# The order of query blocks in the prompt attention of a decoder kernel: 7, 3, 6, 2, 5, 1, 4, 0 instead of 0 to 7

## What is computed

```python
def prompt_attend(q_lat, q_pe, ckv, kpe):
    b, h, s, r = q_lat.shape
    nb = s // Q_BLOCK
    ...
    def block(args):
        qlb, qpb, blk = args
        q_pos = blk * Q_BLOCK + jnp.arange(Q_BLOCK)
        sc = jnp.where(key_pos[None, :] <= q_pos[:, None], mla_scores(qlb, qpb, ckv, kpe), NEG_INF)
        p = jax.nn.softmax(sc, axis=-1).astype(ckv.dtype)
        return jnp.einsum('bhst,btr->bhsr', p, ckv)
```

## Time and profile before

| | us |
|---|---|
| median of 3 runs | 2984.7 (2984.61 to 2985.17) |
| the profiled execution | 2993.13 |
| its span | 2991.0 |
| prompt attention, first scores to last copy | 424.6 to 588.7 |
| TensorE busy | 2811.2 (94% of the span) |
| VectorE, ScalarE, GpSimd busy | 1741.4, 1077.3, 1212.0 |
| mean granted clock of TensorE | 0.973 |

### The profile page before, as it was taken

How to read it: one execution, slowest core, us unless ns; L and a number is a source line. 1 busy time by engine, 2 the same in 40 slices (tenths; PEclk the granted TensorE clock), 3 DMA queues, 4 the chain that set the end, 5 groups by cost and what they waited for, 6 DMA issues and landing times. The chain is left out here.

```text
span 2991.0 us, 60241 instructions
## 1 busy us (share of the span) xinstructions
PE 2811.2 (94%) x24873; PEld 2558.0 (86%) x24873; DVE 1741.4 (58%) x3025; ACT 1077.3 (36%) x2174; POOL 1212.0 (41%) x835
## 2 busy tenths in 40 slices
PE   6999999999999989999999997898989999999996
PEld 4887776666668989999999987877989999999996
DVE  5341245588864876666652276975586666664234
ACT  4511026522225633333320145765553333331111
POOL 2411137733325544444431145784544444433202
PEclk8999989999999999999999998998999999999998
DMA  9555400187743313232382323111232323254422
GB/s 313 185 181 195 137 22 1 52 281 273 278 155 102 118 60 102 103 107 98 102 293 104 126 83 92 43 33 50 83 100 84 109 90 115 89 213 167 148 83 83
DMA packets 232396, 377.87 MB, mean 126 GB/s; under 512 B 14523, under 2 KB 155196, under 8 KB 223669
## 3 DMA queue, kind: packets, MB, share of 16 engines
q1 hardware_dynamic: 200108, 253.95, 25.8%
q0 software_dynamic: 11776, 75.50, 7.2%
q10 hardware_dynamic: 20240, 44.57, 4.1%
HBM read 298.71 MB, written 73.28 MB: 124 GB/s over the span
## 5 line engine op out<-in xcount | busy, mean ns | idle before, releaser
L804 PE MATMUL ps<-HS,w_split 128*128 128x272 f32 x1920 | 272.3, 292 | 23.1 <-POOL w_split L1397 9.8
L804 PEld LDWEIGHTS ps<-HS,w_split 128*128 128x128 f32 x1920 | 253.1, 190 | 28.7 <-ACT sg L1061 14.3
L820 PE MATMUL ps<-HS,w_ring 128*128 128x272 f32 x1920 | 274.7, 290 | 0.0
L820 PEld LDWEIGHTS ps<-HS,w_ring 128*128 128x128 f32 x1920 | 255.4, 190 | 0.0
L2328 PEld LDWEIGHTS ps<-HS_in,w_split 128*128 128x128 f32 x1728 | 223.8, 192 | 28.7 <-issue 18.0
L1799 DVE TENSOR_TENSOR Y<-Y,ps 128x272 f32<-128x272 f32 x256 | 111.9, 437 | 224.9 <-PE ps L820 224.9
L2328 PE MATMUL ps<-HS_in,w_split 128*128 128x272 f32 x1728 | 234.8, 295 | 8.5 <-DVE HS_in L2548 8.4
L1397 POOL TENSOR_TENSOR w_split<-w_raw,w_split 128x512 fp32r<-128x512 f32 x120 | 169.9, 1429 | 156.1 <-ACT w_split L1053 156.1
L775 PE MATMUL ps<-HS,w_ring 128*128 128x272 f32 x1344 | 179.3, 294 | 18.0 <-PEq L3466 11.4
L775 PEld LDWEIGHTS ps<-HS,w_ring 128*128 128x128 f32 x1344 | 175.1, 193 | 20.3 <-POOLq L1446 11.6
L1397 POOL TENSOR_TENSOR w_ring<-w_raw,w_ring 128x512 fp32r<-128x512 f32 x40 | 61.1, 1528 | 270.0 <-ACT w_ring L1053 270.0
(11 more groups left out here) (503 smaller groups left out, 6384.2 us busy)
## 6 DMA issues: line engine op xcount, KB each, us to landing
hid_spill<-hid SPq DMA_DIRECT2D x40, 1088.0 KB, 7.4
w_mod_half<-w_mod_in SPq DMA_DIRECT2D x40, 1024.0 KB, 6.5
HS<-hid_spill ACTq DMA_DIRECT2D x32, 1088.0 KB, 10.7
w_raw<-w_ffn_gate_in SPq DMA_DIRECT2D x44, 512.0 KB, 4.1
w_raw<-w_ffn_up_in SPq DMA_DIRECT2D x44, 512.0 KB, 4.7
w_raw<-w_ffn_down_in SPq DMA_DIRECT2D x44, 512.0 KB, 4.6
x_part<-x_spill SPq DMA_DIRECT2D x54, 272.0 KB, 3.0
x_spill<-Y SPq DMA_DIRECT2D x12, 1088.0 KB, 5.6
```

What stands on the lines that cost most here:

```text
L804: ins = pe.matmul(psum(U.banks(u)[b]), part_slot(j, a)[:, k, :], token_part(n, j, e)[:, k, :], start=(j < 3 and k == 0 and i == 0), stop=( ...
L820: ins = pe.matmul(down_bank(n), slots[DOWN_SLOT[t]][:, a, d * P:(d + 1) * P], hid_cols(k, t, q)[:, e, :], start=(t == lo and j == 0), stop ...
```

## The change

The blocks within a head pair are taken from a table. The wait for the queries and keys of a head, which stood at block 0, now stands at the first block of the pair, whichever that is.

```diff
+BLOCKS = (7, 3, 6, 2, 5, 1, 4, 0)
+
+
 def stage_attention(c, cq, ckv, kq, tab, yb, qlat, qpe, first):
...
         def blk(u):
-            return u // 2 % NQ
+            return BLOCKS[u // 2 % NQ]
...
-                if b == 0:
+                if u // 2 % NQ == 0:
                     pe.wait_ge(q_roped, h + 1)
                     pe.wait_ge(pe_set, h + 1)
```

## The result

The changed kernel takes 2992.59 us in the median of 12 runs (2989.12 to 2997.64), the kernel before 2984.85 in 12 runs taken beside them (2979.38 to 2995.64). The ratio is 1.0024, 95% interval 1.0016 to 1.0032: **slower by 7.2 us, 4.8 to 9.6**. That is clear of no change, and its interval reaches to both sides of the 0.2% (6 us) named before the run. One run on each side of experiment 9 (3456.21 and 6982.73 us) fell in a slow state, and the ratio there leaves them out. The profiled execution took 2994.79 us, span 2992.7, clock 0.975; before it was 2993.13. That pair hides the loss: behind the paged stage's last maximum the program took 2107 us, where the profile of before has 2111. The same code took 2112 us in a second profile of the change. So I compare marks inside the two stages, not spans.

A forecast was written before the change was run, and what follows sets the result against it. TensorE was taken to bound the stage, other engines counting only where late. Fill +2.7, three pairs at +0.85 and drain -2.75 gave +2.5 us, so a median of 2987.2 us, range 2981 to 2993.

The forecast's parts named there:

- rival B: Next stage entered late, so GpSimd's gather of the third page group may land late: +5 to +6.5 us; chance 0.13.
- The waits of the new order: TensorE's waits at junctions 7 to 3, 6 to 2, 5 to 1, 4 to 0: 0.2 to 0.9 us each.
- The pair at +0.85: Each head pair takes about 0.85 us more, 37.5 us: waits of 3.7 to 3.8 us against 2.9 before.
- the prediction on weight loads: In a head pair, weight loads' busy share (23.74 of 36.70 us) shows nearness to the limit better than matmuls' busy time.
- The fill at +2.7: At the stage's start, transposes wait for block 7's long first normalisation: +2.7 us, or +1.7 with the clock effect.
- The drain at -2.75: In the last head pair, short blocks last let the final normalisation end 39.55 us in, not 42.3: -2.75 us.
- Sum at the gather: Fill, three pairs and drain together delay GpSimd's gather behind the last normalisation by 2.5 us.
- so this is hidden by 1.9 us: At the stage's end, entry delayed to about 595.1 us is covered by gathered pages arriving at 597.0.
- It passes whole into the next stage: The +2.5 us at the gather carries fully into the next stage, bound by TensorE after its start.
- Rival A: At the fill, TensorE's half-clock stretch ends 7 to 10 us later: +7 us, 2991.7; chance 0.13.
- Rival C: In each pair, mixed long and short blocks shrink 2.9 us of waits to about 1: -8.6 us, 2976; chance 0.09.
- Rival D: Clock falls inside the loop, one low stretch per pair: +17.5 us, 3002; chance 0.03.

The follow-up runs named there:

- experiment 9: The changed kernel with the last head pair back in the order 0 to 7: 2990.66 us against 2989.1 for the kernel before, ratio 1.0002.
- experiment 1: The changed kernel run again with no edit: 3000.28 us against 2986.36 for the kernel before, one run each.
- experiment 2: The changed kernel with the new order in the first head pair only, the others 0 to 7: 2985.43 us.
- experiment 5: The changed kernel with ScalarE's copy of the values moved behind the odd unit's exponential: 2988.09 us against 2987.34 for the kernel before.
- experiment 8: The changed kernel with VectorE turning the first two page groups ahead of the own-token softmax: 2988.84 us against 2987.34 for the kernel before.
- experiment 3: The changed kernel with the new order in the last head pair only, the others 0 to 7: 2994.26 us.
- experiment 10: The changed kernel with GpSimd normalising only the first half of each row: 2986.77 us against 2989.1 for the kernel before, one run.

## Why the prediction was right and wrong

The time, 2992.6, lies 5.4 above the forecast of 2987.2 and 0.4 inside the upper end of the range. The ratio, 0.24% with an interval of 0.16 to 0.32, lies at the edge of the likeliest case, within 0.2%, and doesn't tell on which side. The cause is the late entry of rival B, priced at +5 to +6.5 and given 0.13; that the sum came as near as it did is partly luck, since its errors had both signs.

- **The waits of the new order: right.** Predicted in turn 0.7, 0.9, 0.3, 0.5, 0.2, 0.7 and 0.4 us. Worked out in the same way from starts in the third pair: 0.71, 0.90, 0.23, 0.45, 0.23, 0.67, 0.42. All seven stand where they were put.
- **The pair at +0.85: the waits of before were too high.** It came to +1.30. The failed step is "So 36.7 - 33.8 = 2.9 us of a pair is waiting". Taking for each kind of piece its shortest time from start to start, TensorE's own work is 34.3 us in every order, not 33.8. Most of the gap is in the values: one block takes 0.37 us, not 0.24. Before, the waits are 0.95 us at block 7's transposes and 0.45 twice and 0.19 twice beside short blocks, with small ones 2.4 in all; after, 3.7. The same count gives 2.0 for 7 down to 0 and 0.9 for 7, 6, 3, 0, 2, 1, 4, 5. The new waits were measured against too bad a past. The count also answers the prediction on weight loads: 2.4 us of idle time lie nearer to the 1.7 that busy matmuls leave of a pair than to the 13.0 that weight loads leave, so for idle time the weight loads' share was not the better measure here.
- **The fill at +2.7: wrong, it was -1.7.** The first pair was to be 3.55 longer and was 0.4 shorter, with 1.3 for the pair itself in it. The sum kept the low stretch at its 20 us. It was 10.2, and again so in the five other profiles that begin with blocks 7 and 3 and have GpSimd's full work (experiments 1, 2, 5, 8 and 9). Ten us more at double the rate are at most 5 us of dense work; 4.4 came. The text named the effect ("if the clock fell later") and allowed it 1 us. The first transpose came at 437.16, not 439.3. The old fill is no fixed quantity either: in experiment 3, with the old order and a low stretch of 13.7, the first pair took 40.8 us and not 43.9.
- **The drain at -2.75: right.** From the last pair's start to the end of its last normalisation: 39.7 us, predicted 39.55, before 42.3.
- **Sum at the gather**: +2.5 predicted, -0.5 measured. That made the place where the forecast broke only worse.
- **"so this is hidden by 1.9 us": the step that decided.** The own-token scores ended 41.0 us into the last pair (said: 40.6), VectorE's chain at 593.44 (said: 594.6). The delay was foreseen, its cover was not there. With the gather issued 3 us sooner than forecast, the pages had landed when VectorE came to them (0.40 us idle at 593.85, where it had idled 6.35), and the entry at 594 became what the stage waits for. Of the chain's end, 1.7 us are the gap of the last section.
- **"It passes whole into the next stage": wrong.** Even +2.5 at the gather was not the quantity that passes. What passes is the entry, +4.8 here and +5.3 at the last maximum. Rival B names the step in between, GpSimd's gather of the third group. By the first profile: entry +4.8, half-clock scores +2.2, so gather +7.0 and turning +7.5; less the 2.98 us for which VectorE had been waiting for TensorE before, +4.5; measured at the second maximum +4.9, at the last one +5.3. Experiment 3 makes the late entry from one pair, 8 and 9 take it away in part and whole. How the delay reaches the second maximum is shown less well: in the first profile the gather's chain and TensorE's second scores end within 0.35 us of each other, in the second TensorE is 3.87 us behind, and experiments 8 and 9 take away its pauses together with the late gather.
- **Rival A** (clock): at the fill the reverse happened. At the seam a part of it did: TensorE, idle for 3.57 us before its first scores, was at 0.52 until 600.0, for most of them. All eight profiles whose last pair ends in blocks 4, 0 or 1, 0 have a second stretch at half clock behind it, 3.4 to 6.8 us long; none of the six others has. What it costs was not measured apart.
- **Rival C** (bubbles fill) fell for this order, as the forecast said, but not as a limit of the kernel: 7, 6, 3, 0, 2, 1, 4, 5 has a pair at 35.20.
- **Rival D**: no clock below 1.00 through the middle pairs of any kernel, with waits of 3.6 to 3.7 us per pair. By the Trainium skill (TensorE: Matmul & The Clock Gate, A second HAM failure mode: psum-queue depth-cycling) it might have swung; the rows do not agree.

Between the 5.3 us at the last maximum and the 7.2 of the medians lies the rest of the program, which took 2107 and 2112 us in the two profiles of the change. Whether 2 us of the median come from there by chance or by cause stays open.

## What to carry to other kernels

Where work of mixed length goes through engines in fixed orders with two or three buffers, do not put a short piece right behind the longest one, look at the joint between groups too, and carry the measured durations through the loop before you choose: steps of one block (7 down to 0) gave 36.28 us, an order with steps of three 35.20. Take a cost from the waits counted one by one, not from a span less a sum. When an edit moves what is queued at a stage's end, follow every chain that gates the next stage, transfers issued inside it among them: an earlier gather helps nothing if the next one's issue waits for the entry. A wait whose removal changes nothing may be hiding behind another; take both away before you write it off.

## What the runs showed of the hardware

- The stretch at half clock at the fill went with what TensorE does first: 20.5 us twice and 13.7 once with one-block scores first (17.1 with half the normalisation), 10.2 with blocks 7 and 3 first, 6.8 with blocks 7 and 6 first, or 7 and 3 with half the normalisation. With one-block scores first the length is not fixed by the code: the fill is the same in all three.
- TensorE pauses in the next stage's second scores, with no semaphore that the profile shows, in the change (both profiles) and in the kernel with the last pair changed, and in none of the eleven other profiles. Two rows of the change:

```profile
607.36 1.10 PE L3186 MATMUL ps<-k_odd,q_rows 32*64 32x256 f32 x4 [0.98 <-issue]
608.79 1.09 PE L3186 MATMUL ps<-k_odd,q_rows 32*64 32x256 f32 x4 [0.33 <-issue]
```

  Without them the second maximum would in this profile still have stood behind VectorE's turning, which ended at 615.52, 0.35 us before it; in the repeat it would not (3.87 us). Their cause is not settled.
- Of the 8.2 us from the own-token scores' end to the end of VectorE's chain (6.6 before), 1.7 lie ahead of its first instruction, put down to "remote"; before the change that gap was 0.05. It stands in the same three profiles as the pauses (1.65 to 1.68 us) and is 0.05 in the ten others that take up these scores in the same place. The two may have one cause; no run was made on it.
- GpSimd's product of half the row took 16.1 us of a pair (experiment 10) against 27.4, so 11.3 us off the engine gave TensorE 1.43: idle engines are not spare ones.
